# The second input projection: rows normed and turned tile by tile, its first two weight tiles multiplied in one pass, one high part moved from ScalarE to VectorE

## The chip, the cores and the metric

The kernel runs on one core of one Trainium2 chip. The metric is the device time of that core in microseconds. The profile is of one execution. Its engines are TensorE (PE; its weight loads are shown apart as PEld), VectorE (DVE), ScalarE (ACT), GpSimd (POOL) and SyncE (SP), which issues most of the loads.

## What is computed

The reference is a stack of three layers over 256 rows of 1024 numbers: a first layer that ends in a mixture of 32 experts, an even layer (sparse latent attention beside a differential attention, then a gated MLP), and an odd layer with the same kind of MLP. The change sits between the first layer and the even one, where this is computed:

```python
x = x + experts(x)                     # end of the first layer
h = rmsnorm(x, norm_mix[0])            # 256 x 1024
y = h @ ev_w_in[0]                     # 1024 x 3048
qa_nope, qa_rope, c_kv, ka_rope, iq, ik, iw, qb, kb, vb = split_cols(y, EVEN_SPLITS)

def rmsnorm(x, g):
    xf = x.astype(jnp.float32)
    y = xf * lax.rsqrt(jnp.mean(xf * xf, axis=-1, keepdims=True) + NORM_EPS)
    return (y * g.astype(jnp.float32)).astype(x.dtype)
```

## The kernel before

The 256 rows are two row tiles (t = 0, 1) of 128 partitions. At the end of the expert layer VectorE adds the last sums to x half by half; ScalarE squares each half and sums it (`end_squares`); VectorE makes mean and reciprocal for both row tiles in one go (L3043 to L3045, `end_recips`); ScalarE takes the root (L2731, `end_roots`); VectorE norms row tile 0 (L3047) and ScalarE row tile 1 (L2549) into `mix`. Each adds one to `rows_ready`. TensorE, which meanwhile does products that nobody reads (`stream`, L139), waits for both.

Then the second input projection begins (the object `pr`, of class `Projection`, with `ready` set since the rows are normed already). TensorE turns the 2 x 8 blocks of 128 x 128 through the identity into PSUM (`begin_pe`, L364; in the trace `later_pB<-con_identity,mix`). ScalarE copies each of the eight column blocks out as float16, scaled by the gain: the high part `sT_hi` (L320). VectorE makes the rest, the low part `sT_lo` (L332).

The weights come in 12 column tiles of 248 or 256 columns, through two slots of `wt` (tile k in slot k % 2). Each is split likewise: the high part by ScalarE (`high_part`, L291, 64 times the weight rounded to float16), the low part by VectorE (`low_part`, L298, which reads the weight and its high part). A product of a tile is three terms, high x high, low x high and high x low, of 8 blocks by 2 row tiles each: 48 products of 128 x 128 by 128 x 248 (`multiply`, L384). ScalarE moves the sums out of PSUM (`move`, L396). The two high parts and two sums in flight also sit in slots k % 2.

What sets the order. Each engine runs its own list of instructions in the order written, and semaphores join them. Tiles 0 and 1 are loaded while the last experts run (`first_loads`, L258). The high part of tile 0 is made between the last squares (`following["high_part"]`). The load of tile k from 2 on (`tile_load`, L278) waits in SyncE for `lo_ready` to reach k - 1, that is for the low part of tile k - 2, and the first of them also for `turned`; loads of the output weights (L521) stand behind it in the same queue. Within `even_in`, VectorE runs `begin_dve` (low part of tile 0, eight low parts of the turned rows, low part of tile 1), then for each k its low part of tile k + 1 and the work on finished columns: first the norm of the latent columns (L3212 to L3219, `ckv_normed`), which TensorE turns in the middle of the product of tile 2 (`turn_latent`, after 14 of its 48 products). GpSimd loads five small tensors for the attention (L3113 to L3120). It does so once `moe_done` has reached 4, to which SyncE, ScalarE, VectorE and TensorE each add one when they leave the expert layer, and once it has cleared that layer's semaphores. TensorE needs these loads after tile 1, for four turns of `uk` (L3283).

The last lines of TensorE and VectorE in the expert layer are these:

```python
stream(T, pB[:, 0, 0:3 * P], keep.marks[:, 0:P], keep.marks[:], 10)
pe.wait_ge(rows_ready, TT)
...
dve.wait_ge(end_roots, 1)
vec.tensor_scalar(out[:, 0, :], x[:, 0, :], x_st[:, 2, 0:1], None, ALU.mult).then_inc(rows_ready, 1)
```

## Time and profile before

| what | value |
|---|---|
| median of 3 runs | 1050.56 us (1049.13 to 1053.37) |
| profiled execution, span from first to last instruction | 1050.0 us |
| mean granted TensorE clock | 0.976 of full |
| busy: TensorE, weight loads | 967.3 us (92%), 693.3 us (66%) |
| busy: VectorE, ScalarE, GpSimd | 587.3 us (56%), 479.8 us (46%), 123.3 us (12%) |
| chain that ended last | TensorE 63%, transfers 13%, VectorE 9%, ScalarE 3% |

The profile gives the span of the profiled execution and no other time of it; the runs' times are from launch to end and some half a microsecond more at the median. In the rows below, times are from the start of the span. A line such as L298 is a line of the kernel, `field` is one large SBUF tensor in which most tiles of the later layers lie, `later_pB` is the PSUM of the later layers and `rw_pB` that of the first. In a timeline, the brackets at the end give how long the engine was idle before the row and what ended that. In the chain of waits, a row DMA is the time from the issue of a transfer to its landing.

### The profile page before, as it was taken

To read this page: it belongs to the slowest core of one execution; us is meant where nothing else is said; L and a number is where in the kernel's file an instruction comes from. 1 tells how busy PE (TensorE), PEld (TensorE's weight loads), DVE (VectorE), ACT (ScalarE), POOL (GpSimd) and SP (SyncE) were. 2 spreads that over 40 slices of the span, in tenths; PEclk is the share of its full clock that TensorE was granted. 3 is DMA by queue.
4 is the path that set the end of the run, shared out by engine and by line. 5 is a ranking of instruction groups with operands and counts; after the bars stand their busy time and mean duration, and the time that the engine had idled before them with its cause. 6 is when DMAs were issued, how large, how long until landed. Compare 5 with 4: busy or idle time off the path is not lost.

```text
span 1050.0 us, 20505 instructions
## 1 busy us (share of the span) xinstructions
PE 967.3 (92%) x8706; PEld 693.3 (66%) x8706; DVE 587.3 (56%) x933; ACT 479.8 (46%) x822; POOL 123.3 (12%) x142
## 2 busy tenths in 40 slices
PE   6899999998756678999999999999999999999996
PEld 5676896554333344887658777776986648777774
DVE  5577888611000004799766554564988856545543
ACT  5566652410000005665664545446657765453442
POOL 5510550000000001014010000000033410000000
PEclk9999999999888899999999999999999999999999
DMA  8756119899999997765044665663725033757611
GB/s 260 228 163 217 43 43 366 341 403 420 421 421 421 421 414 243 261 221 176 26 166 155 207 213 169 218 217 144 235 95 161 2 121 132 242 170 237 217 64 41
DMA packets 108747, 228.68 MB, mean 218 GB/s; under 512 B 7305, under 2 KB 86203, under 8 KB 94075
## 3 DMA queue, kind: packets, MB, share of 16 engines
q1 hardware_dynamic: 105691, 219.38, 57.9%
q0 software_dynamic: 2976, 8.14, 2.7%
q8 instruction: 60, 0.98, 0.4%
q14 instruction: 20, 0.16, 0.0%
HBM read 224.63 MB, written 1.05 MB: 215 GB/s over the span
## 4 chain that ended last, share of the span: by engine, by line
PE 63%; DMA 13%; DVE 9%; ACT 3%; issue 1%; POOL 1%; SPq 1%; DVEq 0%; POOLq 0%
PE later_pB L924 20%; PE later_pB L933 10%; DMA ring<-in_w_down 9%; PE later_pB L880 4%; PE later_pB L384 4%; DMA wt<-in_w_down 3%; PE rw_pB L1404 2%; PE rw_pB L1425 2%; DVE field L298 2%; PE later_pB L912 2%; PE rw_pB L2476 1%; DMA wt<-in_ev_w_in 1%; PE rw_pB L1433 1%; PE later_pB L4059 1%; PE rw_pB L2242 1%
## 5 line engine op out<-in xcount | busy, mean ns | idle before, releaser
L924 PE MATMUL later_pB<-field 128*128 128x256 f16 x1920 | 212.9, 273 | 0.0
L924 PEld LDWEIGHTS later_pB<-field 128*128 128x128 f16 x1920 | 187.7, 98 | 25.6
L753 DVE SCALAR_TENSOR_TENSOR field<-field 128x2048 f16<-128x2048 f32 x84 | 153.8, 1869 | 56.8 <-ACT field L648 56.8
L648 ACT ACTIVATE field<-field 128x2048 f16<-128x2048 f32 x84 | 126.4, 1567 | 15.5 <-DMA field<-in_ffn_w_up 9.2
L933 PE MATMUL later_pB<-field 128*128 128x512 f16 x528 | 117.7, 379 | 0.6 <-DVE field L753 0.6
L384 PE MATMUL later_pB<-field 128*128 128x256 f16 (+2 forms) x960 | 114.9, 274 | 0.6
L384 PEld LDWEIGHTS later_pB<-field 128*128 128x128 f16 x960 | 94.2, 99 | 13.5 <-ACT field L320 1.8
L933 PEld LDWEIGHTS later_pB<-field 128*128 128x128 f16 x528 | 51.6, 98 | 58.8 <-issue 1.5
L1404 PE MATMUL rw_pB<-ring,kept 128*32 128x256 f32 x816 | 64.9, 409 | 25.0 <-DMA ring<-in_w_up 21.9
L1336 DVE TENSOR_TENSOR rw_mu_a<-rw_pB,rw_mu_a 128x256 f32<-128x256 f32 x8 | 3.4, 425 | 119.6 <-PE rw_pB L1404 119.6
L1404 PEld LDWEIGHTS rw_pB<-ring,kept 128*32 128x32 f32 x816 | 35.6, 118 | 50.0 <-issue 36.1
L769 DVE SCALAR_TENSOR_TENSOR field<-later_pB,field 128x512 f32<-128x512 f32 x22 | 15.2, 691 | 91.9 <-ACT field L666 91.9
L298 DVE SCALAR_TENSOR_TENSOR field<-wt,field 128x2048 f16<-128x2048 f32 (+2 forms) x22 | 52.7, 2398 | 13.6 <-ACT field L291 13.0
L666 ACT ACTIVATE field<-later_pB 128x512 f32<-128x512 f32 x22 | 13.1, 597 | 102.6 <-PE later_pB L924 102.5
L291 ACT ACTIVATE field<-wt 128x2048 f16<-128x2048 f32 (+2 forms) x22 | 42.1, 1918 | 7.7 <-DMA wt<-in_ev_w_in 5.9
L880 PE MATMUL later_pB<-field 128*128 128x512 f16 x192 | 43.9, 384 | 0.0
L1425 PE MATMUL rw_pB<-ring,rw_mu_a 128*32 128x512 f32 x216 | 34.1, 667 | 9.5 <-DMA ring<-in_w_down 5.0
L1295 ACT ACTIVATE rw_mu_a<-rw_pB 128x256 f32<-128x256 f32 x8 | 3.1, 388 | 74.4 <-PE rw_pB L1462 74.4
L384 PE MATMUL in_pY<-ring 128*128 128x256 f16 (+1 forms) x288 | 34.1, 271 | 3.2 <-ACT ring L291 1.7
L1433 PE MATMUL rw_pB<-rw_few_y,rw_mu_a 128*128 128x512 f32 x64 | 29.8, 606 | 7.4 <-ACT rw_few_y L1304 6.5
L666 ACT ACT_TABLE_LOAD x8 | 10.3, 1283 | 56.3 <-PE later_pB L924 44.9
L384 PEld LDWEIGHTS in_pY<-ring 128*128 128x128 f16 x288 | 27.1, 98 | 9.6 <-ACT ring L291 2.3
(592 smaller groups left out, 1594.3 us busy)
## 6 DMA issues: line engine op xcount, KB each, us to landing
ring<-in_w_up SPq DMA_DIRECT2D x26, 1024.0 KB, 26.6
ring<-in_w_gate SPq DMA_DIRECT2D x25, 1024.0 KB, 21.7
ring<-in_w_down SPq DMA_DIRECT2D x23, 1024.0 KB, 26.4
field<-in_ffn_w_down SPq DMA_DIRECT2D x22, 1024.0 KB, 5.0
field<-in_ffn_w_gate SPq DMA_DIRECT2D x20, 1024.0 KB, 7.6
field<-in_ffn_w_up SPq DMA_DIRECT2D x20, 1024.0 KB, 9.9
wt<-in_ev_w_in SPq DMA_DIRECT2D x9, 1024.0 KB, 5.7
wt<-in_od_w_in SPq DMA_DIRECT2D x9, 1024.0 KB, 5.6
```

Source lines behind the costliest of these rows:

```text
L291: self.nc.scalar.activation(self.w_hi[:, k % 2, :, 0:n], self.wt[:, k % 2, :, 0:n], ACT.Copy, scale=W_SCALE).then_inc(self.hi_ready, 1)
L298: self.nc.vector.scalar_tensor_tensor(self.w_lo[:, k % 2, :, 0:n], self.wt[:, k % 2, :, 0:n], W_SCALE, self.w_hi[:, k % 2, :, 0:n], ALU.mu ...
L384: ins = self.nc.tensor.matmul(self.pY[:, slot, t, 0:n], x[:, c, t * P:(t + 1) * P], w[:, slot, c, 0:n], start=(term == 0 and c == 0), stop ...
L648: copy = lambda o, i, scale=1.0: nc.scalar.activation(o, i, ACT.Copy, scale=scale)
L666: nc.scalar.activation(gated[:, s, :], pG[:, s, :], ACT.Silu, scale=1.0 / W_SCALE).then_inc(silu_done, 1)
L753: return nc.vector.scalar_tensor_tensor(out, whole, scale, hi, ALU.mult, ALU.subtract)
L880: return nc.tensor.matmul(pY[:, t, half_of(n)], source[:, c, t * P:(t + 1) * P], by[:, c, half_of(n)], start=(c == 0 and term == 0), stop= ...
L924: ins = T.matmul(p[:, s, j * SEQ:(j + 1) * SEQ], w[:, s, m, c, j::NJ], h[:, c, :], start=(n == 0), stop=(n == 3 * KC - 1))
L933: return T.matmul(pY[:, t, half_of(half)], h[:, s, at:at + P], w[:, s, j, half_of(half)], start=False, stop=stop, skip_group_check=True)
L1404: ins = nc.tensor.matmul(into[i * CAP:(i + 1) * CAP, 0:D_EXPERT], h[:, c, i * CAP:(i + 1) * CAP], held[:, c * D_EXPERT:(c + 1) * D_EXPERT] ...
L1425: ins = nc.tensor.matmul(pD[i * CAP:(i + 1) * CAP, half, :], hidT[:, j, i * CAP:(i + 1) * CAP], held[:, at:at + 512], start=(j == 0), stop ...
L1433: ins = nc.tensor.matmul(pY[:, t, half, :], into_tokens[:, g, t * P:(t + 1) * P], y[:, half * 512:(half + 1) * 512], start=(g == 0), stop= ...
```

## The change

The rows are normed tile by tile: VectorE makes mean and reciprocal for row tile 0 and then for row tile 1, ScalarE the two roots; VectorE norms row tile 0 and the right half of row tile 1, ScalarE the left half (new semaphore `row_left`). TensorE turns row tile 0 as soon as it is ready and then row tile 1, as the last thing of its expert layer, and the products ahead of it that nobody reads are six and not ten. The high part of weight tile 1 is made by VectorE with one `tensor_scalar`, ahead of its low part of tile 0. TensorE multiplies tiles 0 and 1 in one pass (`multiply_two`): high x high block by block as ScalarE's copies arrive, with tile 1 two blocks behind, then the other two terms of tile 0 (high x low, low x high) and of tile 1 (low x high, high x low).

```diff
+    def begin_two_dve(self, dve):
+        n = self.tiles[1][1]
+        dve.wait_ge(self.hi_ready, 1)
+        dve.wait_ge(*self.raw_in_of(1))
+        self.nc.vector.tensor_scalar(self.w_hi[:, 1, :, 0:n], self.wt[:, 1, :, 0:n], W_SCALE, None, ALU.mult).then_inc(self.hi_ready, 1)
+        dve.wait_ge(self.hi_ready, 2)
+        self.begin_dve(dve)
...
+    def multiply_two(self, pe):
+        def add(k, c, term, first, last):
+            x, w = ((self.sT_hi, self.w_hi), (self.sT_lo, self.w_hi), (self.sT_hi, self.w_lo))[term]
+            n = self.tiles[k][1]
+            for t in range(TT):
+                ins = self.nc.tensor.matmul(self.pY[:, k, t, 0:n], x[:, c, t * P:(t + 1) * P], w[:, k, c, 0:n], start=first,
+                                            stop=last, skip_group_check=True)
+            return ins
+        pe.wait_ge(self.hi_ready, 1)
+        for c in range(KC + 2):
+            if c < KC:
+                pe.wait_ge(self.high_T, c + 1)
+                add(0, c, 0, c == 0, False)
+            if c == 2:
+                pe.wait_ge(self.hi_ready, 2)
+            if c >= 2:
+                add(1, c - 2, 0, c == 2, False)
+        for k, order in enumerate(((2, 1), (1, 2))):
+            for term in order:
+                if term == 2:
+                    pe.wait_ge(self.lo_ready, k + 1)
+                for c in range(KC):
+                    if k == 0 and term == 1:
+                        pe.wait_ge(self.low_T, c + 1)
+                    ins = add(k, c, term, False, term == order[-1] and c == KC - 1)
+            ins.then_inc(self.product, 1)
...
-            stream(T, pB[:, 0, 0:3 * P], keep.marks[:, 0:P], keep.marks[:], 10)
-            pe.wait_ge(rows_ready, TT)
+            stream(T, pB[:, 0, 0:3 * P], keep.marks[:, 0:P], keep.marks[:], 6)
+            following["turn"](pe, ((rows_ready, 1),), 0)
+            following["turn"](pe, ((rows_ready, 2), (row_left, 1)), 1)
...
-            act.wait_ge(end_recips, 1)
-            nc.scalar.activation(x_st[:, 2, :], x_st[:, 1, :], ACT.Sqrt).then_inc(end_roots, 1)
-            act.wait_ge(end_roots, 1)
-            copy(out[:, 1, :], x[:, 1, :], x_st[:, 2, 1:2]).then_inc(rows_ready, 1)
+            for t in range(TT):
+                act.wait_ge(end_recips, t + 1)
+                nc.scalar.activation(x_st[:, 2, t:t + 1], x_st[:, 1, t:t + 1], ACT.Sqrt).then_inc(end_roots, 1)
+            act.wait_ge(end_roots, 2)
+            copy(out[:, 1, 0:512], x[:, 1, 0:512], x_st[:, 2, 1:2]).then_inc(row_left, 1)
...
-            dve.wait_ge(end_squares, len(X_ORDER))
...
+            for t in range(TT):
+                dve.wait_ge(end_squares, len(X_ORDER) - TT + t + 1)
+                link(vec.tensor_reduce(x_st[:, 0, t:t + 1], end_halves[:, t, :], AX_X, ALU.add))
+                link(vec.tensor_scalar(x_st[:, 0, t:t + 1], x_st[:, 0, t:t + 1], 1.0 / D, EPS, ALU.mult, ALU.add))
+                vec.reciprocal(x_st[:, 1, t:t + 1], x_st[:, 0, t:t + 1]).then_inc(end_recips, 1)
             dve.wait_ge(end_roots, 1)
             vec.tensor_scalar(out[:, 0, :], x[:, 0, :], x_st[:, 2, 0:1], None, ALU.mult).then_inc(rows_ready, 1)
+            dve.wait_ge(end_roots, 2)
+            vec.tensor_scalar(out[:, 1, 512:], x[:, 1, 512:], x_st[:, 2, 1:2], None, ALU.mult).then_inc(rows_ready, 1)
...
-        pr.begin_pe(pe)
...
+        pr.multiply_two(pe)
+        for k in range(1, n_tiles):
+            if k > 1:
+                pr.multiply(pe, k, {2: turn_latent, n_tiles - 1: turn_keys}.get(k))
...
                     def _(pe):
                         mixing.tensor(pe)
                         pe.sem_inc(moe_done, 1)
-                        wait_alone(pe, old_done, cleared, 1)
```

The new `begin_two_act` is `begin_act` without its last line, the high part of tile 1; `turn_rows` is one row tile of `begin_pe`.

The order on VectorE from the end of the expert layer to the latent norm, before (`rw_x_st` holds the row statistics, `mix` the normed rows, `wt` the raw weight tile, the reading of `later_pB` is the low part of the turned rows):

```order
L3043 TENSOR_REDUCE rw_x_st<-rw_end_halves 128x2
L3044 TENSOR_SCALAR rw_x_st<-rw_x_st 128x2
L3045 RECIPROCAL rw_x_st<-rw_x_st 128x2
L3047 TENSOR_SCALAR mix<-x,rw_x_st 128x1024
L298 SCALAR_TENSOR_TENSOR field<-wt,field 128x8x248
L332 SCALAR_TENSOR_TENSOR field<-later_pB,in_gain,field 128x256 x8
L298 SCALAR_TENSOR_TENSOR field<-wt,field 128x8x248 x2
L3212 ISA field<-field 128x128
```

and in the changed kernel:

```order
L3105 TENSOR_REDUCE rw_x_st<-rw_end_halves 128x1
L3106 TENSOR_SCALAR rw_x_st<-rw_x_st 128x1
L3107 RECIPROCAL rw_x_st<-rw_x_st 128x1
L3105 TENSOR_REDUCE rw_x_st<-rw_end_halves 128x1
L3106 TENSOR_SCALAR rw_x_st<-rw_x_st 128x1
L3107 RECIPROCAL rw_x_st<-rw_x_st 128x1
L3109 TENSOR_SCALAR mix<-x,rw_x_st 128x1024
L3111 TENSOR_SCALAR mix<-x,rw_x_st 128x512
L389 TENSOR_SCALAR field<-wt 128x8x248
L298 SCALAR_TENSOR_TENSOR field<-wt,field 128x8x248
L332 SCALAR_TENSOR_TENSOR field<-later_pB,in_gain,field 128x256 x8
L298 SCALAR_TENSOR_TENSOR field<-wt,field 128x8x248 x2
```

Five instructions are new on VectorE: three of the statistics, half a row tile (L3111) and the high part of weight tile 1 (L389), which stands between the norm and the low part of tile 0.

The same stretch of ScalarE, before:

```order
L2731 ACTIVATE rw_x_st<-rw_x_st 128x2
L2549 ACTIVATE mix<-x,rw_x_st 128x1024
L320 ACTIVATE field<-later_pB,in_gain 128x256 x8
L291 ACTIVATE field<-wt 128x8x248
L396 ACTIVATE field<-later_pB 128x2x248
L291 ACTIVATE field<-wt 128x8x248
```

and in the changed kernel:

```order
L2792 ACTIVATE rw_x_st<-rw_x_st 128x1 x2
L2609 ACTIVATE mix<-x,rw_x_st 128x512
L381 ACTIVATE field<-later_pB,in_gain 128x256 x8
L455 ACTIVATE field<-later_pB 128x2x248
L291 ACTIVATE field<-wt 128x8x248
```

The first of the two L291, the high part of tile 1, is gone from here; the one that stays is that of tile 2, behind the move of tile 0's sums.

## Rows read from the trace of the kernel before

**Rows 1.** the chain of waits, start us, us, what, 409 to 426 us

```profile
410.13 1.16 ACT mix L2549
411.29 0.29 issue
411.58 1.54 PE later_pB L364 x12
413.12 8.49 DMA wt<-in_ev_w_in
...
421.63 1.87 ACT field L291
...
423.52 2.23 DVE field L298
```

**Rows 2.** VectorE in order of time: start, us, operation [idle before, releaser]

```profile
409.30 0.16 DVE L3043 TENSOR_REDUCE rw_x_st<-rw_end_halves 128x2 f32<-128x4 f32 x1 [0.79 <-ACT mix L2728]
...
410.14 0.75 DVE L3047 TENSOR_SCALAR mix<-x,rw_x_st 128x1024 f32<-128x1024 f32 x1 [0.27 <-ACT rw_x_st L2731]
410.80 2.22 DVE L298 SCALAR_TENSOR_TENSOR field<-wt,field 128x1984 f16<-128x1984 f32 x1
413.99 3.23 DVE L332 SCALAR_TENSOR_TENSOR field<-later_pB,in_gain,field 128x256 f16<-128x256 f32 x8 [0.97 <-ACT field L320]
```

**Rows 3.** GpSimd in order of time

```profile
412.49 0.82 POOL L3113 DMA_DIRECT2D field<-in_ev_w_uk  x1 [266.61 <-PEq L146]
413.30 0.90 POOL L3115 DMA_DIRECT2D field<-in_ev_w_uv  x1
```

**Rows 4.** ScalarE in order of time

```profile
413.03 3.03 ACT L320 ACTIVATE field<-later_pB,in_gain 128x256 f16<-128x256 f32 x8 [1.75 <-PE later_pB L364]
415.90 1.91 ACT L291 ACTIVATE field<-wt 128x1984 f16<-128x1984 f32 x1
420.67 0.58 ACT L396 ACTIVATE field<-later_pB 128x496 f32<-128x496 f32 x1 [2.86 <-PE later_pB L384]
```

**Rows 5.** busy time of each engine in six stretches

```profile
core 0: us, PE busy (x) PEld busy (x) DVE busy (x) ACT busy (x) POOL busy (x), PEclk, DMA share, GB/s
386.50:411.00 24.50, 18.54 (x124) 8.64 (x124) 5.29 (x11) 8.43 (x16) 0.00 (x0) 1.00 0.85 308
...
414.00:418.00 4.00, 3.49 (x24) 2.25 (x25) 3.38 (x9) 3.81 (x7) 1.81 (x4) 1.00 1.02 320
418.00:421.00 3.00, 3.00 (x31) 2.77 (x30) 2.07 (x1) 0.33 (x1) 0.00 (x0) 1.00 1.04 210
...
425.75:489.00 63.25, 62.47 (x555) 54.30 (x553) 58.06 (x107) 40.60 (x51) 16.09 (x12) 1.00 0.58 186
489.00:501.70 12.70, 11.89 (x83) 6.69 (x84) 11.76 (x40) 8.93 (x31) 0.00 (x0) 1.00 1.00 322
...
514.00:522.00 8.00, 7.40 (x55) 5.74 (x54) 5.15 (x18) 6.04 (x17) 0.00 (x0) 0.83 0.00 0
```

**Rows 6.** TensorE products in order of time

```profile
413.65 12.06 PE L384 MATMUL later_pB<-field 128*128 128x248 f16 x96
...
488.95 1.09 PE L3258 MATMUL later_pB<-con_identity,field 128*128 128x128 f32 x8 [0.34 <-POOLq L3126]
...
501.68 0.50 PE L3514 MATMUL later_pB<-field,low 128*128 128x384 bf16 x2 [0.50 <-DVE field L3106]
```

**Rows 7.** VectorE groups by shape: busy us, mean ns, idle before

```profile
L441 DVE TENSOR_SCALAR mix<-x,in_stats 128x512 f32<-128x512 f32 x2 | 1.0, 486 | 0.5 <-ACT in_stats L430 0.5
...
L3105 DVE TENSOR_SCALAR field<-field 128x384 f32<-128x384 f32 x1 | 0.4, 360 | 0.0
...
L1860 DVE TENSOR_SCALAR ring<-ring 128x128 f32<-128x128 f32 x1 | 0.2, 226 | 0.0
...
L1329 DVE CAST rw_router_g<-pick 128x64 f16<-128x64 f32 x1 | 0.2, 189 | 0.0
```

**Rows 8.** the chain of waits further on, a load of a later weight tile

```profile
449.55 5.65 DMA wt<-in_ev_w_in
```

More of the change, by code:

```diff
@@ L366, in begin_pe, with turn_rows, begin_two_act @@
                     ins.then_inc(self.turned, 1)
+    def turn_rows(self, pe, t):
+        for c in range(KC):
+            at = c % 2 * SEQ + t * P
+            ins = self.nc.tensor.transpose(self.pT[:, c // 2, at:at + P], self.xn[:, t, c::KC], self.con["identity"])
+            if t == TT - 1 and c % 2:
+                ins.then_inc(self.turned, 1)
+    def begin_two_act(self, act):
+        act.wait_ge(self.gain_in, 16)
+        for c in range(KC):
+            act.wait_ge(self.turned, c // 2 + 1)
+            self.nc.scalar.activation(self.sT_hi[:, c, :], self.pT[:, c // 2, c % 2 * SEQ:(c % 2 + 1) * SEQ], ACT.Copy,
+                                      scale=self.gcol[:, c:c + 1]).then_inc(self.high_T, 1)
@@ new lines, in begin_two_dve, with raw_in_of @@
+    def begin_two_dve(self, dve):
[5 more added lines that the diff above has]
+        self.begin_dve(dve)
+    def raw_in_of(self, k):
+        return self.w_in[k % 2], 16 * (k // 2 + (self.first is None and self.late is None))
+    def multiply_two(self, pe):
[19 more added lines that the diff above has]
+                    pe.wait_ge(self.lo_ready, k + 1)
+                for c in range(KC):
+                    if k == 0 and term == 1:
+                        pe.wait_ge(self.low_T, c + 1)
+                    ins = add(k, c, term, False, term == order[-1] and c == KC - 1)
+            ins.then_inc(self.product, 1)
@@ L2003 @@
               "centred", "gap", "experts_chosen", "counted"]
-END_NAMES = ["vlink", "gate_exps", "xn_hi", "xn_lo", "flag_set", "x_summed", "end_squares", "end_recips", "end_roots", "rows_ready"]
+END_NAMES = ["vlink", "gate_exps", "xn_hi", "xn_lo", "flag_set", "x_summed", "end_squares", "end_recips", "end_roots", "rows_ready", "row_left"]
 V_LEVELS = 2
@@ L2091, in first_mix @@
          x_squares, x_recips, x_roots, normed, xn_turned, xT_left, xT_right, routed, centred, gap, experts_chosen, counted) = tail_sems
-        vlink, gate_exps, xn_hi, xn_lo, flag_set, x_summed, end_squares, end_recips, end_roots, rows_ready = end_sems
+        vlink, gate_exps, xn_hi, xn_lo, flag_set, x_summed, end_squares, end_recips, end_roots, rows_ready, row_left = end_sems
         small = Room(router_g[:].rearrange("p c n -> p (c n)"))
@@ L3130, in scalar @@
         two = lambda ap: ap.rearrange("p n s -> p (n s)")
-        pr.begin_act(act)
+        pr.begin_two_act(act)
         for k in range(n_tiles):
@@ L3203, in weigh @@
             dve.sem_inc(rel_used, 1)
-        pr.begin_dve(dve)
+        pr.begin_two_dve(dve)
         for k in range(n_tiles):
@@ L3275, in turn_keys @@
                 ins.then_inc(kb_turned, 1)
-        for k in range(n_tiles):
-            pr.multiply(pe, k, {2: turn_latent, n_tiles - 1: turn_keys}.get(k))
+        pr.multiply_two(pe)
+        for k in range(1, n_tiles):
+            if k > 1:
+                pr.multiply(pe, k, {2: turn_latent, n_tiles - 1: turn_keys}.get(k))
             if k == 1:
@@ L4312, in next_high_part, with next_turn @@
                     stages["pr"].high_part(act, 0)
-                following.update(loads=next_loads, high_part=next_high_part)
+                def next_turn(pe, ready, t):
+                    if t == 0:
+                        wait_alone(pe, old_done, cleared, 1)
+                    for sem, count in ready:
+                        pe.wait_ge(sem, count)
+                    stages["pr"].turn_rows(pe, t)
+                following.update(loads=next_loads, high_part=next_high_part, turn=next_turn)
                 with nc.Block(no_gpsimd_drain=True) as block:
```

3 lines of the change are left out of this document (removed).

## The prediction

> **What bounds the kernel now.** I read the page first. TensorE is busy 92% of the span, but that is a mean over stages, so I looked for the stage that the change touches: the end of the expert layer and the first three weight tiles of the second input projection, 408 to 426 us of the profiled execution. The chain of waits for that stretch [rows 1] shows the norm of the rows on ScalarE (1.16 us for one row tile), twelve of the sixteen turns on TensorE, then a transfer of 8.49 us: weight tile 2 (counted from 0), which lands at 421.63. After it come its high part on ScalarE (1.87) and its low part on VectorE (2.23). The products of tiles 0 and 1 are not on this chain, though TensorE runs them from 413.65 to 425.7 without a gap worth naming [rows 6].
>
> Next, what follows. From 425.75 to 489.0 VectorE is busy 58.06 of 63.25 us, and 11.76 of the 12.70 after that; TensorE is busy 62.47 of 63.25 [rows 5]. The two go side by side: when the keys are turned at 488.95 TensorE has waited only 0.34 us for GpSimd, and at 501.68 it waits 0.50 us for VectorE [rows 6]. VectorE starts this stretch with the low part of tile 2, in order; the norm of the latent columns stands behind it, and TensorE needs that norm in the middle of the product of tile 2. So a shift of that low part moves both engines, and almost nothing in the 76 us behind it can take the shift up. The question is only when tile 2 lands.
>
> Tile 2's load is issued at 413.12. The program lets it go when a turn has been counted and VectorE has made the low part of tile 0, because that frees the slot. In the profile both come at the same moment: the low part runs 410.80 to 413.02 [rows 2], the chain has the turns until 413.12 [rows 1]. The landing is then slow. A load of the same kind with little beside it takes 5.65 us [rows 8]; this one takes 8.49. The windows say why: 320 GB/s in 414 to 418 and 210 GB/s in 418 to 421, at a full DMA share in both [rows 5]. What shares the engines then is GpSimd's own loads, issued from 412.49 and 413.30 [rows 3].
>
> **The change part by part.**
>
> *Rows normed one by one, on two engines.* VectorE now does three small operations per row tile in place of three for both. The three take 0.57 us (from 409.30; the common root and the norm follow 0.27 us after them), and the first set fits into the 0.79 us in which VectorE waits for ScalarE's last square [rows 2]: nothing. The norm of row tile 0 then no longer waits 0.27 us for the common root: it starts at about 409.90, not 410.14, and ends at 410.65. VectorE's next instruction can start 0.66 us after the start of this one (410.80 less 410.14), so at 410.56. Then VectorE norms half of row tile 1: 0.49 us [rows 7], with the same overlap about 0.40, so VectorE is free at 410.96, 0.16 later than now. ScalarE does the other half, about 0.63 in place of 1.16, from 410.13: ready at 410.76.
>
> *Turning in two steps.* With the 0.29 us between the norm's end and the first turn (411.29 to 411.58 in [rows 1]), the first eight turns start at 410.94. The sixteen take 2.01 us as before, the second eight find their rows ready (411.1), and the first bank is complete after ten: 410.94 + 10 x 0.11 + 0.27, or 412.3. ScalarE's eight copies then start about 0.7 us before the 413.03 of now [rows 4]. Six in place of ten filler products (0.18 us each, on nobody's path) end before the turns begin.
>
> *High part of tile 1 on VectorE.* This takes 1.91 us off ScalarE, behind its copies [rows 4]; ScalarE waits 2.86 us right after, so by itself it gains nothing there. It makes the high part of tile 1 early, which the joint product needs. On VectorE it is one multiplication by a constant, 1984 elements, float32 in SBUF to float16. No row shows that size. From below: 226 ns for 128 elements and 360 for 384 give 0.523 ns an element, and 226 + 1856 x 0.523 = 1.20 us. From above: the low part of the same shape, two tensors in, takes 2.22 us [rows 2]. A cast of 64 elements to float16 takes 189 ns; the line through the two float32 rows gives 192 there [rows 7], so the narrow output costs nothing, and I take 1.20. The Trainium skill, "VectorE: DVE Perf Modes", the perf-mode tier table, has one-source float32 operations between SBUF operands at two elements a cycle, 1227 ns for 2048; by that page it would be an estimate of 1.2 us too, and no run here shows this form.
>
> What matters is its place: it stands **ahead of** the low part of tile 0, and that low part is what lets tile 2's load go. VectorE: 410.96 + 1.20 = 412.16, the low part 412.20 to 414.42, the load issued 0.1 later at 414.5. That is 1.4 us later than now. The turns, counted by 412.3, no longer matter for it.
>
> *GpSimd's loads move too.* They are behind a count that all engines add to when they leave the expert layer, and TensorE now adds to it after its sixteen turns and not before them. Now: norm's end 411.29, first load 412.49, so 1.20 us between. After: the last turn is issued at about 410.94 + 1.75 = 412.7, and the first load at 413.9, again 1.4 us later. Tile 2's load and GpSimd's loads keep their distance, so I keep the 8.49 us: tile 2 lands at 414.5 + 8.5 = 423.0. The bounds are 5.65 us if the two hardly meet (420.2) and, with the slow form of the high part, 415.5 + 8.5 = 424.0. On the other side the Trainium skill, "DMA: Bandwidth & Descriptors", queues, rings and completion order, says that each DMA engine takes turns between the queues that have work, a packet from each. The trace agrees in that the rate falls to 210 GB/s while GpSimd's loads are under way; by that rule only the order of the two matters, which is rival 1 below.
>
> *The joint product.* It takes away the wait in which TensorE is held to ScalarE's copies: now one product of 0.11 us for each copy of 0.37 (seven times), after it two for each of the first two copies and four for each later one, 0.42 us, which ScalarE outruns. TensorE starts at about 412.95 and does 96 products at 0.105, with 0.3 us of waits: done at 423.4, against 425.5 now [rows 6], so 2.1 us sooner. The low parts it asks for are there: tile 0 at 414.4, wanted at 416.7; the turned low parts by 417.7, wanted at 418.4; tile 1 at 419.9, wanted at 421.7. But TensorE then needs tile 2's high part, which ends at 423.0 + 1.9 = 424.9. So it stands idle for about 1 us, and then waits again for the latent norm. The whole 2.1 us is lost at this point.
>
> **The sum.** Low part of tile 2 on VectorE: now 423.52, after it 424.9. That is +1.4 us (high part of tile 1 +1.20, halved norm +0.16, waits +0.05), passed on by both full engines to the end. The profiled execution has a span of 1050.0 us and the median of the three runs is 1050.56, so 0.56 lies around the span and stays. 1050.56 + 1.4 = 1052.0.
>
> **The rivals.**
> 1. *Tile 2's load slips past GpSimd's.* If GpSimd's loads move by more than 1.4 us (TensorE adds to the count late), tile 2 takes nearer 5.65 us and lands at 420.2. The high part then waits for the product of tile 0 (64 products after 412.95, so 420.0) and the move of it (0.58): 420.7 + 1.9 = 422.6, against 423.5 now: -0.9 us, 1049.7. For it: only about 0.7 us separates the two. Against it: the two shifts come out equal.
> 2. *The high part costs what the low part costs,* 2.22 us. Then the load goes at 415.5, more of it beside GpSimd's, and the low part of tile 2 starts at 425.9: +2.4, 1053.0. Against it stand the rows of 64, 128 and 384 elements.
> 3. *TensorE's clock falls.* The place is the new idle stretch before tile 2, 423.4 to 424.9. The granted clock is 0.83 of full in 514 to 522, with TensorE 7.40 of 8.00 us busy in short work [rows 5]: some 2.7 us at the 1.2 GHz level, the rest at 2.4, a loss of 1.4 us. Two such stretches on a path that both engines fill cost 2.8 us on top of the forecast: 1054.8, slower from the first one on. Against it: in 386.5 to 411.0 TensorE was idle a quarter of the time (18.54 us busy of 24.50) and the clock stayed at full.
> 4. *The change does what it says.* TensorE's 2.1 us reach the end: 1048.5. For it: TensorE is as full as VectorE behind 425.75. Against it: it can't start tile 2 without the load, and the load goes later.
>
> **How the numbers follow.** Forecast 0.60, rival 1 0.16, rival 2 0.10, rival 3 0.05, rival 4 0.05; 0.04 for what I don't see. A measurement of this kernel tells about 0.5% (5.3 us) from no change, and the three runs shown lie 4.2 us apart. None of the cases moves the time by 5.3 us alone. The range takes in all four with the scatter of the runs, 1047.5 to 1055.0. Faster by over 0.5%: 0.06. Slower by over 0.5%: 0.06. Within: 0.88.
>
> **What would show it.** In the profile after: the multiplication on VectorE at about 1.2 us, right ahead of the low part of tile 0; tile 2's load issued near 414.5 and landed near 423.0, counted from the same point of the expert layer; the first turn some 0.6 us earlier; the 96 products ending near 423.4, then an idle TensorE that waits for ScalarE's high part; GpSimd's first load about 1.4 us later. The latent norm and all behind it about 1.4 us later against the last sums of the expert layer. The prediction is wrong if tile 2's load lands in under 7 us, or if TensorE goes straight from tile 1 into tile 2.

## The result, and the profile after

The changed kernel takes 1052.55 us at the median of its 21 runs, the kernel before 1049.61 in the same set. The ratio of the means, with one disturbed run of 1973.93 us left out, is 1.0023, with a 95% interval of 1.0014 to 1.0031: 2.4 us slower (1.5 to 3.3). The forecast was +1.4 us and no change by the bound of 0.5%. The verdict holds, though all four rivals of the prediction lay inside that bound too, and the size is short by 1 us.

In what follows, times of different kernels are compared from one common point, the start of VectorE's last sum into x in the expert layer. It lies at 407.83 in the profile of before and at 407.32 in that of after; up to there both do the same work. From VectorE in order of time, before:

```profile
407.83 0.69 DVE L1322 TENSOR_TENSOR x<-x,rw_pB 128x512 f32<-128x512 f32 x1 [0.17 <-PE rw_pB L1433]
```

The same view of after, for [rows 2]:

```profile
407.32 0.69 DVE L1381 TENSOR_TENSOR x<-x,rw_pB 128x512 f32<-128x512 f32 x1 [0.17 <-PE rw_pB L1492]
...
409.26 0.73 DVE L3109 TENSOR_SCALAR mix<-x,rw_x_st 128x1024 f32<-128x1024 f32 x1
409.91 0.48 DVE L3111 TENSOR_SCALAR mix<-x,rw_x_st 128x512 f32<-128x512 f32 x1
410.30 1.19 DVE L389 TENSOR_SCALAR field<-wt 128x1984 f16<-128x1984 f32 x1
411.52 2.22 DVE L298 SCALAR_TENSOR_TENSOR field<-wt,field 128x1984 f16<-128x1984 f32 x1
...
424.91 2.23 DVE L298 SCALAR_TENSOR_TENSOR field<-wt,field 128x1984 f16<-128x1984 f32 x1 [5.90 <-ACT field L291]
...
451.97 2.28 DVE L298 SCALAR_TENSOR_TENSOR field<-wt,field 128x2048 f16<-128x2048 f32 x1
459.15 2.29 DVE L298 SCALAR_TENSOR_TENSOR field<-wt,field 128x2048 f16<-128x2048 f32 x1 [0.89 <-ACT field L291]
...
466.92 5.36 DVE L3265 SCALAR_TENSOR_TENSOR field<-field 128x128 f32<-128x128 f32 x8
```

The low part of tile 0 now starts at 411.52, 4.20 after the common point, against 2.97 before (410.80 less 407.83): 1.23 later. The chain of waits of after shows what that does, for [rows 1]; its last row stands in [rows 8] for before:

```profile
413.84 9.15 DMA wt<-in_ev_w_in
423.00 0.02 issue
423.02 1.86 ACT field L291
424.89 0.02 issue
424.91 2.23 DVE field L298
...
450.94 6.24 DMA wt<-in_ev_w_in
```

Tile 2's load goes 1.23 us later (6.52 after the common point, 5.29 before) and takes 9.15 in place of 8.49 us. VectorE's low part of tile 2 starts 17.59 after it, not 15.69: 1.90 later. From there VectorE does the same work in the same time: 27.06 us from 424.91 to 451.97, and also 27.06 before (423.52 to 450.58). Then the load of the later tile takes 6.24 us against 5.65 (+0.59), and a group of eight operations 5.36 against 5.19 (+0.17). The sum is 1.90 + 0.59 + 0.17 = 2.66. The product that [rows 6] shows at 501.68 stands at 503.85 in the profile after: 96.53 against 93.85 after the common point, 2.68 later, in line with the 2.4 measured. Of before, VectorE in order of time:

```profile
450.58 2.29 DVE L298 SCALAR_TENSOR_TENSOR field<-wt,field 128x2048 f16<-128x2048 f32 x1
...
464.94 5.19 DVE L3201 SCALAR_TENSOR_TENSOR field<-field 128x128 f32<-128x128 f32 x8
```

TensorE in order of time, for [rows 6]:

```profile
410.05 2.03 PE L372 MATMUL later_pB<-con_identity,mix 128*128 128x128 f32 x16
412.14 10.55 PE L404 MATMUL later_pB<-field 128*128 128x248 f16 x96
422.53 0.60 PE L3348 MATMUL later_pB<-con_identity,field 128*128 128x128 f32 x4
424.93 1.66 PE L443 MATMUL later_pB<-field 128*128 128x248 f16 x14 [1.80 <-ACT field L291]
428.77 0.44 PE L3322 MATMUL later_pB<-con_identity,field 128*128 128x128 f32 x2 [2.18 <-DVE field L3283]
...
503.85 0.50 PE L3579 MATMUL later_pB<-field,low 128*128 128x384 bf16 x2 [0.50 <-DVE field L3170]
```

The turns start at 2.73 after the common point, 1.02 earlier than before (411.58 less 407.83 is 3.75), and the 96 products are done 10.55 us after their start, against 12.06. TensorE then waits 1.80 us for tile 2's high part and 2.18 for the latent norm. GpSimd's loads, for [rows 3], and the stretches that answer to [rows 5] (us, busy time of PE, PEld, DVE, ACT, POOL, clock, DMA share, GB/s):

```profile
411.67 0.82 POOL L3177 DMA_DIRECT2D field<-in_ev_w_uk  x1 [266.33 <-issue]
412.48 0.90 POOL L3179 DMA_DIRECT2D field<-in_ev_w_uv  x1
```

```profile
414.00:418.00 4.00, 4.00 (x41) 3.70 (x39) 4.00 (x9) 0.55 (x2) 0.99 (x2) 1.00 0.78 173
418.00:421.00 3.00, 3.00 (x31) 2.78 (x29) 1.01 (x1) 0.58 (x1) 0.00 (x0) 1.00 1.03 359
...
424.00:427.00 3.00, 1.66 (x14) 1.29 (x14) 2.09 (x1) 0.88 (x1) 0.00 (x0) 1.00 1.08 385
427.00:430.00 3.00, 1.23 (x11) 1.11 (x12) 2.20 (x10) 2.01 (x3) 0.00 (x0) 0.96 0.81 286
430.00:433.00 3.00, 3.00 (x16) 2.23 (x15) 2.15 (x3) 3.00 (x5) 0.00 (x0) 0.50 0.76 247
...
515.70:523.70 8.00, 7.40 (x64) 5.58 (x61) 5.78 (x20) 6.63 (x19) 0.00 (x0) 1.00 0.00 1
```

After the two waits the granted clock is 0.50 of full, the level of 1.2 GHz, from about 430 to 433. And the fall that [rows 5] has in 514 to 522 is not in the profile after (its last row). That fall costs time, as the part on the frame of the sum shows below, so the two spans, 1050.5 and 1050.0, can't be compared as they stand. The profiled execution of after took 1052.55 us with a span of 1050.5, so 2.05 us lie around the span, not the 0.56 that the prediction took; over all runs that list both, the difference is 1.72 to 2.22.

### The profile page after: what moved, and what is told of

Same layout as the page of the kernel before. It is cut to its first block, busy times and chain, and to the rows that moved or that the text cites. A ratio compares the mean times of both kernels' runs of the same rounds, so it can differ in the third digit from the quotient of the medians.

```text
span 1050.5 us, 20505 instructions
## 1 busy us (share of the span) xinstructions
PE 965.1 (92%) x8702; PEld 692.9 (66%) x8702; DVE 588.8 (56%) x938; ACT 477.6 (45%) x822; POOL 122.5 (12%) x142
## 4 chain that ended last, share of the span: by engine, by line
PE 64%; DMA 10%; DVE 10%; ACT 3%; SPq 3%; issue 2%; POOL 0%; DVEq 0%
PE later_pB L983 20%; PE later_pB L992 10%; PE later_pB L939 4%; DMA ring<-in_w_down 4%; PE later_pB L443 4%; PE rw_pB L1463 3%; DMA ring<-in_w_up 3%; DMA ring<-in_w_gate 3%; DVE field L298 3%; PE later_pB L971 2%; SPq L1331 2%; PE rw_pB L1484 2%; PE rw_pB L2535 1%; DMA wt<-in_ev_w_in 1%; PE rw_pB L1492 1%
## 5 line engine op out<-in xcount | busy, mean ns | idle before, releaser
L983 PEld LDWEIGHTS later_pB<-field 128*128 128x128 f16 x1920 | 187.7, 98 | 25.6
L443 PE MATMUL later_pB<-field 128*128 128x256 f16 (+2 forms) x864 | 105.0, 277 | 1.8 <-ACT field L291 1.8
L443 PEld LDWEIGHTS later_pB<-field 128*128 128x128 f16 x864 | 85.7, 100 | 13.6 <-ACT field L291 2.0
L992 PEld LDWEIGHTS later_pB<-field 128*128 128x128 f16 x528 | 51.6, 98 | 58.8 <-issue 1.5
L291 ACT ACTIVATE field<-wt 128x2048 f16<-128x2048 f32 (+2 forms) x21 | 40.2, 1917 | 9.9 <-DMA wt<-in_ev_w_in 7.8
```

The lines of the kernel that those rows point to most:

```text
L291: self.nc.scalar.activation(self.w_hi[:, k % 2, :, 0:n], self.wt[:, k % 2, :, 0:n], ACT.Copy, scale=W_SCALE).then_inc(self.hi_ready, 1)
L443: ins = self.nc.tensor.matmul(self.pY[:, slot, t, 0:n], x[:, c, t * P:(t + 1) * P], w[:, slot, c, 0:n], start=(term == 0 and c == 0), stop ...
L983: ins = T.matmul(p[:, s, j * SEQ:(j + 1) * SEQ], w[:, s, m, c, j::NJ], h[:, c, :], start=(n == 0), stop=(n == 3 * KC - 1))
L992: return T.matmul(pY[:, t, half_of(half)], h[:, s, at:at + P], w[:, s, j, half_of(half)], start=False, stop=stop, skip_group_check=True)
```

## The experiments

Every edit is made to the changed kernel. Each was timed in five rounds beside the kernel before. The changed kernel was not timed again with them, so a comparison with its 1.0023 goes across sets of runs. In the table, all but the ratio is from one profile each, in us: the issue of tile 2's load, VectorE's low part of tile 2, and the product of 128 x 384 count from the common point.

| kernel | ratio to before, 95% | load issued | load takes | low part of tile 2 | product 128 x 384 |
|---|---|---|---|---|---|
| before | | 5.29 | 8.49 | 15.69 | 93.85 |
| after | 1.0023 (1.0014 to 1.0031) | 6.52 | 9.15 | 17.59 | 96.53 |
| low part first | 0.9995 (0.9983 to 1.0007) | 5.29 | 6.7 | 15.07 | 93.05 |
| high part back on ScalarE | 0.9996 (0.9978 to 1.0014) | 5.30 | 7.73 | 14.94 | 93.08 |
| rows tile by tile alone | 1.0002 (0.9989 to 1.0015) | 5.30 | 7.1 | 14.35 | 92.88 |
| high part made twice | 1.0017 (1.0006 to 1.0028) | 7.62 | 7.55 | 17.08 | 95.31 |
| GpSimd's loads after the low part | 1.0017 (1.0005 to 1.0028) | 6.53 | 9.35 | 17.79 | 96.70 |
| tile 2's load alone | 1.0041 (1.0026 to 1.0056) | 6.52 | 5.43 | 14.39 | 98.46 |
| the same, high part of tile 2 first | 1.0041 (1.0024 to 1.0058) | 6.51 | 5.29 | 13.97 | 97.42 |
| TensorE kept busy | 1.0029 (1.0012 to 1.0046) | 6.52 | 8.99 | 17.42 | 99.26 |
| TensorE kept busy, again | 1.0036 (1.0020 to 1.0053) | 6.52 | 9.37 | 17.80 | 100.45 |
| uv and lambda late | 0.9991 (0.9980 to 1.0003) | 5.29 | 6.72 | 13.92 | 92.25 |

**Low part first.** The same multiplication, but VectorE makes the low part of tile 0 before it:

```diff
-        dve.wait_ge(self.hi_ready, 1)
+        self.low_part(dve, 0)
         dve.wait_ge(*self.raw_in_of(1))
         self.nc.vector.tensor_scalar(self.w_hi[:, 1, :, 0:n], ...).then_inc(self.hi_ready, 1)
...
-        self.begin_dve(dve)
...
```

The lines that follow are those of `begin_dve` without its first, the low part of tile 0.

> The changed kernel, but VectorE makes the low part of tile 0 first and the high part of tile 1 behind it. Theory (tile 2's load is let go late and lands behind GpSimd's loads): the load goes some 1.2 us earlier than in the changed kernel, near 412.6 in its time, now about 0.9 us behind GpSimd's first load (0.6 before, 2.2 in the changed kernel), and takes 8.5 to 9 us. VectorE's low part of tile 2 starts 1.2 to 1.9 us earlier, and the kernel is 1.2 to 2.5 us faster than the changed one, so within 1 us of the kernel before. Rival (the loss is TensorE's: idle and clock, whatever the load): TensorE gets tile 1's high part 0.7 us late, so no gain, 1052 to 1053. Rival (landing is fixed by GpSimd's loads and not by the issue): the landing moves by less than 0.3 us and so does the time.

The slowdown is gone: 0.9995. The load is issued at 5.29, as before the change, and takes 6.7 us, not the 8.5 to 9 expected. The product of 128 x 384 stands 3.5 us earlier than in the changed kernel. The work is the same, only its order on VectorE differs. Chain of waits and TensorE of this kernel:

```profile
409.68 2.06 DVE field L298
411.75 1.18 DVE field L389
...
419.80 1.86 ACT field L291
421.69 2.23 DVE field L298
```

```profile
411.44 1.03 PE L410 MATMUL later_pB<-field 128*128 128x248 f16 x6
412.98 9.70 PE L410 MATMUL later_pB<-field 128*128 128x248 f16 x90 [0.51 <-DVE field L389]
```

The load is no longer on the chain. The high part of tile 2 needs the slot of tile 0's high part, which the joint product gives back late, and stands behind the move of tile 0's sums.

**High part back on ScalarE.** The joint product stays. ScalarE makes the high part of tile 1, between its half of the norm and its copies of the turned rows:

```diff
+        self.high_part(act, 1)
...
-        pr.begin_two_dve(dve)
+        pr.begin_dve(dve)
```

> The changed kernel, but the high part of tile 1 is made by ScalarE, between its half of the norm and its copies of the turned rows; VectorE goes straight to the low part of tile 0. The joint product stays. Theory (only VectorE's multiplication ahead of that low part did the harm): tile 2's load is issued 5.3 us after the last sum (6.5 in the changed kernel), the copies and with them the products start 0.6 us later (5.5 against 4.8), the low part of tile 2 starts at 15 to 15.7, and the time is that of the kernel before within 1 us, 1.5 to 2.5 us below the changed one. Rival (the joint product is at fault): as the changed kernel.

0.9996. Neither of the two kernels in which nothing stands ahead of the low part shows a slowdown, so the multiplication in that place is its cause, as far as intervals of 0.12 to 0.18% either way can tell. The joint product by itself brings nothing that can be measured.

**Rows tile by tile alone.** Both the high part and the two products in the order of before:

```diff
-        pr.begin_two_act(act)
+        pr.begin_act(act)
...
-        pr.begin_two_dve(dve)
+        pr.begin_dve(dve)
...
-        pr.multiply_two(pe)
-        for k in range(1, n_tiles):
-            if k > 1:
-                pr.multiply(pe, k, {2: turn_latent, n_tiles - 1: turn_keys}.get(k))
+        for k in range(n_tiles):
+            pr.multiply(pe, k, {2: turn_latent, n_tiles - 1: turn_keys}.get(k))
```

> Only the first part of the change: rows normed and turned tile by tile, six filler products; the high part of tile 1 on ScalarE behind its copies and tiles 0 and 1 multiplied one after the other, as before. Theory: VectorE goes from the norm (which ends at the same point as before within 0.1 us) straight to the low part of tile 0, so tile 2's load is issued 5.3 us after the last sum, as before, and lands after 7 to 8.5 us; the low part of tile 2 at 15.1 to 15.9 (before 15.7, changed 17.6), the time that of the kernel before within 1 us. Rival (the tile by tile norm with its half row tile on VectorE costs something itself): low part of tile 2 later than 16, 1051 or more.

1.0002. The low part of tile 2 starts at 14.35, ahead of the 15.1 expected at the earliest, and the product of 128 x 384 comes about 1 us sooner than before (92.88 against 93.85), which the timed runs can't tell from nothing.

**High part made twice.** A second multiplication of the same size, into a place that is overwritten later, to test whether a delay on VectorE is passed on one for one:

```diff
+        self.nc.vector.tensor_scalar(self.w_lo[:, 1, :, 0:n], self.wt[:, 1, :, 0:n], W_SCALE, None, ALU.mult)
         dve.wait_ge(self.hi_ready, 2)
```

> The changed kernel with the multiplication for the high part of tile 1 done twice on VectorE, ahead of the low part of tile 0 (1.2 us of doubled work). Theory (VectorE's time ahead of that low part goes one for one into the end): 1.2 us slower than the changed kernel, near 1053.8. If GpSimd's loads are nearly through by then, the landing may lose less than 1.2: between 0.5 and 1.2. Rival (work hidden in the idle of VectorE, which is 5.9 us long before tile 2's low part): no change.

It is not passed on. The load goes 1.10 us later than in the changed kernel (7.62), yet it takes 7.55 and not 9.15 us, and the low part of tile 2 starts at 17.08, half a microsecond earlier. The ratio of 1.0017 does not exceed that of the change, where the expectation was 1.2 us more. Tile 2's load now stands 3.28 us behind GpSimd's first (7.62 less 4.34). In the changed kernel it is 2.17 (6.52 less 4.35), before it was 0.63 (413.12 less 412.49).

**GpSimd's loads after the low part,** to bring back the small distance:

```diff
         link = Link(pool, glink)
+        pool.wait_ge(pr.lo_ready, 1)
```

> The changed kernel, but GpSimd's five loads wait until VectorE has made the low part of tile 0, so they are issued when tile 2's load is, and not 2.2 us before it. Theory: tile 2's load then runs ahead of most of GpSimd's traffic and takes 5.7 to 7.5 us in place of 9.15: it lands near 420 to 421, TensorE hardly waits for the high part (unless its four turns of uk wait for the late loads, up to 424), and the kernel is 1.5 to 3 us faster than the changed one. Rival (the load is slow for another reason, the output weights behind it or its own short pieces): still about 9 us and no change in time.

With its loads issued from 6.73 on, right behind tile 2's at 6.53, the load took 9.35 us: no shorter. The 5.7 to 7.5 us expected did not come. So it isn't the distance alone that sets the load's time. In the three kernels ahead of these two it is 0.95 us each time (5.29 or 5.30 less 4.34 or 4.35), and the load took 6.7, 7.73 and 7.1.

**Tile 2's load alone.** GpSimd waits until the load has landed; the turns of `uk`, for which TensorE would wait, go into the product of tile 2:

```diff
         link = Link(pool, glink)
+        pool.wait_ge(pr.w_in[0], 2 * 16)
...
         def turn_latent(done):
             if done == 5:
+                pe.wait_ge(rows_in, 5 * 16)
+                for n in range(4):
+                    nc.tensor.transpose(sc[:, 1, n * P:(n + 1) * P], uk[:, n, :], ident)
...
-                pe.wait_ge(rows_in, 5 * 16)
-                for n in range(4):
-                    nc.tensor.transpose(sc[:, 1, n * P:(n + 1) * P], uk[:, n, :], ident)
```

> The changed kernel, but GpSimd's five loads wait until tile 2's load has landed, and the four turns of uk stand in the middle of tile 2's product (beside the turn of the latent columns) so that nothing waits for them. Theory (GpSimd's loads slow tile 2's load): it takes 5.7 us in place of 9.15, lands 12.2 us after the last sum of the expert layer (15.7 in the changed kernel), the low part of tile 2 starts near 14.6 (17.6), and the kernel is about 3 us faster than the changed one, 0 to 1 us faster than the one before. Rival (the load is slow of itself or by the output weights behind it): 8.5 us or more, and at best 0.5 us gained.

The load takes 5.43 us, so 3.7 of its 9.15 us are the company of GpSimd's loads. Alone means without these: two loads of output weights, 512 KB each, are issued right behind it here as in all the kernels, as SyncE in order of time shows:

```profile
414.13 1.14 SPq L580 DMA_DIRECT2D field<-in_ev_w_out  x2
```

But it wins nothing: 1.0041. The chain of waits of this kernel:

```profile
413.55 5.43 DMA wt<-in_ev_w_in
418.97 0.29 issue
419.26 0.81 POOL field L3178
...
422.04 7.68 DMA field<-in_ev_subln
429.72 0.04 issue
429.77 1.12 PE later_pB L3331 x4
```

The five loads are now late themselves. A column of 0.5 KB, the last of them, takes 7.68 us beside the next weight tiles, and TensorE stands idle for 5.88 us until 429.77. In 429 to 436 its granted clock is then 0.64:

```profile
429.00:436.00 7.00, 6.23 (x39) 5.26 (x40) 5.13 (x11) 3.53 (x5) 0.00 (x0) 0.64 0.80 265
```

**The same, with the high part of tile 2 ahead of the move of tile 0's sums** on ScalarE (`pr.high_part(act, 2)` goes before the loop).

> As load_alone, and ScalarE makes the high part of tile 2 before it moves the sums of tile 0, not behind. In load_alone the high part stands behind that move (0.58 us), so the low part of tile 2 starts 0.5 us earlier here, near 14.1 us after the last sum: the fastest of all, 1 to 1.8 us below the kernel before. If load_alone's load still lands later than the product of tile 0, the move is out of the way already and this one is the same as load_alone.

1.0041 again. The low part of tile 2 starts 0.42 us sooner (13.97), and the load that lands late is the same one (6.67 us).

**TensorE kept busy.** Products that nobody reads, 8 ahead of tile 2's product and 9 in it, at the wait for the latent norm, fill the two idle stretches, so that the clock doesn't fall. (In the edit the nine stand first, in the function that tile 2's product calls.)

```diff
+        def keep_on(n):
+            for _ in range(n):
+                nc.tensor.matmul(sc[:, 3, :], pr.sT_hi[:, 0, 0:P], pr.sT_hi[:, 0:2, :].rearrange("p c s -> p (c s)"), start=True, stop=True,
+                                 skip_group_check=True)
...
+                keep_on(9)
...
+                keep_on(8)
```

> The changed kernel with 8 unread products of 128x512 (0.21 us each) behind the turns of uk and 9 before the wait for the latent norm, so that TensorE is not idle for 1.8 and 2.2 us there. Theory (those idle stretches bring the 1.2 GHz level of 429.8 to 433.2 with them, worth 0.8 us at 501): the granted clock stays at 1.00 in 427 to 436 and the kernel is 0.5 to 1 us faster than the changed one. Rival (the clock falls there or elsewhere by chance): the level falls at another place and the time does not change by more than 0.3 us.

> The kernel of the experiment with products that nobody reads in TensorE's two idle stretches before and in tile 2, once more, since its profile held a stretch in which eight operations of VectorE took 8.07 us in place of 5.2. If the clock's fall near 430 us is 0.8 us of the changed kernel's 2.4, and that stretch was chance, this kernel stands at 1.0015 of before, its clock stays at full, and the product of 128 x 384 starts some 95.7 us after VectorE's last sum into x. If the stretch comes again, the added products or their place bring it about, and the ratio stays at 1.003.

The clock stays at full, as this stretch of the first of the two profiles shows, yet the ratio is 1.0029, and 1.0036 in the repeat, no better than the 1.0023 of the change (the intervals overlap):

```profile
428.00:431.00 3.00, 3.00 (x30) 2.60 (x27) 2.15 (x3) 3.00 (x5) 0.00 (x0) 1.00 0.82 276
```

The fall of the clock near 430 us was worth nothing: VectorE takes 27.05 and 27.06 us from the low part of tile 2 to the point that the changed kernel reaches in 27.06 with the fall. VectorE sets the pace there, and TensorE gets back in its own waits what it lost. What the kernel loses comes behind it. The load of the later tile takes 6.86 and 7.37 us (6.24 in the changed kernel, 5.65 before), and then this, from VectorE and GpSimd of the repeat in order of time:

```profile
466.45 9.12 DVE L3265 SCALAR_TENSOR_TENSOR field<-field 128x128 f32<-128x128 f32 x8
```

```profile
467.13 1.27 POOL L1547 TENSOR_TENSOR field<-field,con_rope 128x512 f32<-128x512 f32 x1 [53.96 <-ACT field L455]
468.49 1.28 POOL L1548 TENSOR_TENSOR field<-field,con_rope 128x512 f32<-128x512 f32 x1
469.84 1.33 POOL L1549 TENSOR_TENSOR field<-field,con_rope 128x512 f32<-128x512 f32 x1
471.25 1.28 POOL L1550 TENSOR_TENSOR field<-field,con_rope 128x512 f32<-128x512 f32 x1
```

The group of eight took 9.12 us (8.07 in the first profile, 5.36 in the changed kernel). In the changed kernel GpSimd starts its six operations 2.47 us after the group, and the fourth of them is the one that is held up, while VectorE makes the next low part:

```profile
469.39 1.27 POOL L1547 TENSOR_TENSOR field<-field,con_rope 128x512 f32<-128x512 f32 x1 [54.40 <-ACT field L455]
...
473.49 3.21 POOL L1550 TENSOR_TENSOR field<-field,con_rope 128x512 f32<-128x512 f32 x1
```

In the repeat it starts 0.68 us after the group, none of its operations is held up, and VectorE pays. Where GpSimd begins only behind the group, as in the kernel with tile 2's load alone (at 471.20), the same eight operations take 3.20 us:

```profile
468.30 3.20 DVE L3266 SCALAR_TENSOR_TENSOR field<-field 128x128 f32<-128x128 f32 x8
```

The Trainium skill, "SBUF — State Buffer", section "Who interferes with whom", says that a VectorE instruction with two inputs in SBUF and a GpSimd instruction that reads SBUF exclude each other for their whole length. These rows agree. That the stretch came in both profiles speaks against chance, but two profiles are few, and the runs of the first lie far apart (1048.24 to 1057.48). Why the load ahead of it takes longer in these kernels stays open.

**uv and lambda late.** The best that the runs pointed to: rows tile by tile alone, only the loads that are wanted first beside tile 2's, and the high part of tile 2 ahead of the move.

```diff
-        nc.gpsimd.dma_start(uv[:]..., w_uv...).then_inc(rows_in, 16)
         nc.gpsimd.dma_start(kv_col[:], cols(kv_gain)).then_inc(rows_in, 16)
-        nc.gpsimd.dma_start(e.lam..., spread(lam...)).then_inc(rows_in, 16)
         nc.gpsimd.dma_start(e.subln[:], cols(subln)).then_inc(rows_in, 16)
+        pool.wait_ge(rows_in, 3 * 16)
+        pool.wait_ge(pr.w_in[0], 2 * 16)
+        nc.gpsimd.dma_start(uv[:]..., w_uv...).then_inc(rows_in, 16)
+        nc.gpsimd.dma_start(e.lam..., spread(lam...)).then_inc(rows_in, 16)
...
-        pr.begin_two_act(act)
+        pr.begin_act(act)
+        pr.high_part(act, 2)
...
```

Not shown are the other edits of the rows-alone kernel and the waits of ScalarE and TensorE. They now ask for three of GpSimd's loads, and TensorE asks for all five only ahead of its products with `uv`.

> Rows normed and turned tile by tile alone; both high parts and both products in the order of before. Of GpSimd's five loads the three that are wanted first (uk, two columns) go as before, uv and lambda only when weight tile 2 has landed; ScalarE makes the high part of tile 2 before it moves the sums of tile 0. Tile 2's load is issued 5.3 us after VectorE's last sum into x. If contention with GpSimd's loads sets its landing, it takes 5.4 to 6.2 us (7.1 with all five beside it), the high part starts when the product of tile 0 ends, at 12.0, and the low part at 13.9, 0.5 us before that of the kernel with the rows alone (14.35): about 1049.0, 0.9995 of before. The rival: uv and lambda now run beside tile 3's load, which lands later, and what was won is given back there: 1.000 or above.

0.9991 (0.9980 to 1.0003): the lowest ratio of all, and still not told from before. It does not decide between the gain expected (0.9995) and the rival (1.000). The low part of tile 2 stands at 13.92 as expected, 1.77 us earlier than before, and the product of 128 x 384 1.60 earlier (92.25). But the load took 6.72 us and not the 5.4 to 6.2 expected, and the next one 8.86:

```profile
411.21 6.72 DMA wt<-in_ev_w_in
417.95 1.87 ACT field L291
419.84 2.23 DVE field L298
422.09 8.86 DMA wt<-in_ev_w_in
```

## Why the prediction came out as it did

**The high part on VectorE: right.** 1.19 us against 1.20 forecast. The bound from above, the 2.22 us of rival 2, fell.

**The norm by halves: nearly right.** ScalarE's half took 0.72 us, not 0.63. The norm of row tile 0 starts 1.94 after the common point, against 2.07 forecast (409.90 less 407.83). So the low part of tile 0 is 1.23 us late and not 1.4, and so is the load. The first turn comes 1.02 us earlier and not 0.64: it starts 0.06 us after VectorE's norm of row tile 0 ends (409.26 + 0.73, then 410.05), where the prediction took the 0.29 that it had read behind ScalarE's norm.

**GpSimd's loads move too: wrong.** This step failed. The prediction put the first of them 1.20 us behind the last turn's issue and so 1.4 us later. It came at 4.35 after the common point, against 4.66 before: 0.31 earlier. It starts at 411.67 and the turns end at 412.08 (410.05 + 2.03), so what TensorE adds to the count did not come after its turns had run. VectorE's norm ends at 410.39, 1.28 before the load, and nearly the same distance was taken from the norm's end on ScalarE before (1.20). In the seven other profiles in which GpSimd's first load is left free it is 1.27 or 1.28 too, while the load lies anything from 0.41 to 0.57 ahead of the end of the turns. So it goes with the end of the norm, though which engine's entry comes last isn't shown.

The two transfers, then, did not keep their distance, and with it fell the ground on which the 8.49 us were kept: the load took 9.15. The landing at 15.67 after the common point is 1.89 later, where the forecast had 1.4.

The company of GpSimd's loads costs tile 2's load 3.7 of its 9.15 us, and the four kernels that issue it at 6.52 or 6.53 with these loads beside it all have 8.99 to 9.37, also the one with a distance of 0.20 us the other way (6.73 less 6.53). So the distance alone does not set it. The packets that each queue moved, counted from the issue of tile 2's load, show more (the hardware queue, q1, carries tile 2 and the output weights behind it, the software queue, q0, GpSimd's loads):

| kernel | load takes, us | hardware queue, first 3 us | software queue, first 3 us | software queue until the landing |
|---|---|---|---|---|
| tile 2's load alone | 5.43 | 414 packets | none | none |
| rows tile by tile alone | 7.1 | 412 packets | 0.27 MB | 0.66 MB |
| before | 8.49 | 318 packets | 0.26 MB | 0.66 MB |
| after | 9.15 | 17 packets | 0.55 MB | 0.60 MB |
| high part made twice | 7.55 | 80 packets | 0.38 MB | 0.38 MB |
| GpSimd's loads after the low part | 9.35 | 325 packets | none | 0.66 MB |

In the changed kernel tile 2's load is hardly served in its first 3 us, while GpSimd's go through. With the high part made twice it meets only what is left of them, 0.38 MB, and is shorter. With GpSimd's loads issued behind it, it starts well and meets them all further on. An even turn-taking between the queues, a packet from each, to which the prediction pointed, does not show in the first 3 us of after: 17 packets of the hardware queue stand against 199 of the software queue. So what kept it back in the changed kernel was that it came behind GpSimd's loads and waited for them. This is read from the packets; no run puts the two loads back to the distance of before with all else unchanged. Why one and the same 0.66 MB cost 1.7 us in one kernel and 3.9 in another (7.1 and 9.35, less 5.43) stays open.

**Passed on by both full engines: right in the first 27 us, too little behind.** 27.06 us there and 27.06 before, to a hundredth. Then two more terms that the sum hadn't, 0.59 for the later load and 0.17 for the eight operations beside GpSimd. The prediction took every duration behind tile 2 as fixed. Once VectorE shifts against GpSimd and the loads, they aren't. Nor is a delay ahead of the load passed on to its landing one for one, as was expected of the kernel with the high part made twice: there 1.10 us more gave −0.51 at the low part of tile 2.

**TensorE's gain is lost: right.** Forecast were 96 products ending 2.1 us sooner and about 1 us of idle time. (The 2.1 is counted from 425.5; by [rows 6] they end at 425.71 before, and the forecast of 423.4 means 2.3.) From the common point they end at 15.37 (412.14 + 10.55 less 407.32) against 17.88 (413.65 + 12.06 less 407.83): 2.5 sooner. The wait was 1.80 us, and 2.18 more for the latent norm.

**The rivals.** Rival 1, the load slips past: its condition never came about, since GpSimd's loads moved the other way. Where the load was made to run alone, the low part of tile 2 came 1.30 us earlier than before (14.39), more than the 0.9 of rival 1, and the kernel was slower by 0.4% all the same, since GpSimd's loads then came late. Rival 2, a high part of 2.22 us: ruled out by the 1.19. Rival 3, the clock falls: it did, some 5 us behind the idle stretch that rival 3 named, and cost nothing. It had the right event with the wrong price, since the path there is VectorE's and not TensorE's. Rival 4, a gain of 2.1 us: ruled out by the ratio.

**The frame of the sum.** 0.56 us around the span was a span of one execution against the median of others. In the result of after it is 2.05. The profiled execution of before also had a clock fall that costs: from the product of 128 x 384 to the end it needs 548.32 us, the changed kernel 546.65. The other profiles bear this out. Five of the twelve have a clock of 0.50 some 18 to 20 us behind that product (before, GpSimd's loads after the low part, the two with tile 2's load alone, the repeat of TensorE kept busy), and exactly these five need 548.2 to 548.3 us from there to the end; the other seven need 546.5 to 546.7. TensorE kept busy has the fall in one of its two profiles only, so the kernel alone does not decide it. The two errors lie in the level and not in the difference, so they did not hurt here. That 1052.0 lies so near the measured 1052.55 is in part luck: the three runs of before that it starts from have a median 0.95 us above that of the 21.

## What to carry to other kernels

An operation that takes an engine's spare time costs what stands behind it in that engine's queue. Here 1.2 us of VectorE stood ahead of the instruction that frees a weight slot, and the same operation one place later cost nothing that could be measured. Before work is moved onto an engine, find the instruction there that lets the next transfer go, and put the moved work behind it. When two full engines pass a shift on, the shift is only the first term. Here 1.90 us of it became 2.68, with the high part made twice 1.39 became 1.46, and of a gain of 1.34 with the rows alone 0.97 was left. Whatever shares a resource with a third party (loads, VectorE beside GpSimd) has to be priced again at its new place.

## What the runs showed of the hardware

- A load of 992 KB took 5.29 and 5.43 us without GpSimd's loads beside it, and 6.7 to 9.37 us beside five of them that together carry some 640 KB. In the longest, 8.99 to 9.37, it was hardly served in its first 3 us (15 to 41 packets), or met GpSimd's loads further on. With `uk` and two columns beside it, it was 6.72.
- A load of 0.5 KB took 6.67 and 7.68 us while weight tiles were under way.
- TensorE's clock fell to half for about 3.4 us after waits of 1.80 and 2.18 us in close order, and stood at 0.64 on average in the 7 us that follow a wait of 5.88. The first of these cost nothing (27.06 us of VectorE's work with it, 27.05 and 27.06 without). Another fall to half, some 18 us behind the product of 128 x 384, went with 1.6 us more to the end in the five profiles that have it.
- VectorE and GpSimd: eight operations of VectorE took 3.20 us with none of GpSimd's beside them and 5.17 to 9.12 with them, the most where GpSimd began 0.68 us after; one operation of GpSimd took 1.28 or 3.21.
